# Moving fill units, gate work and mixed rows in a two-block transformer kernel: the recurrence, the MLA pairs and the first half of WO0

## What is computed

```python
proj = rms_norm(x, g_mix) @ w_in      # q_mla, c_kv, k_rope, q/k/v/a/r of GLA, q_mem, gate_logits
kv   = rms_norm(c_kv, g_ckv) @ w_ukv  # k_nope and v of MLA
o_mla = causal_block_attention(q_full, k_full, v_mla, 192 ** -0.5)      # 8 heads
og    = gla_chunked(qg, kg, vg, log_a)                                  # 4 heads, a decayed recurrence
o_gla = rms_norm(og, g_gla_out) * silu(r_gla)
o_mem = softmax attention over mem                                      # 4 heads
gates = sigmoid(gate_logits + b_gate).reshape(B, S, 3, D_MODEL)
y = gates[..., 0, :] * o_mla + gates[..., 1, :] * o_gla + gates[..., 2, :] * o_mem
x = x + y @ w_o
```

## Time and profile before

| | us |
|---|---|
| median of 3 runs | 972.43 (970.01 to 975.63) |
| profiled execution | 970.61 |
| its span, first to last instruction | 969.0 |
| PE busy in it | 919.7 |
| DVE busy | 736.7 |
| ACT busy | 540.2 |
| mean granted clock of PE (1 is 2.4 GHz) | 0.989 |

### The profile page before, as it was taken

One profiled execution on the slowest core, in us unless ns is written; L12 is line 12 of the kernel. 1 busy time (PEld: TensorE's weight loads), 2 busy tenths in 40 slices (PEclk: granted clock), 3 DMA queues, 4 the chain that ended last, 5 costly groups with the idle time before them and its releaser, 6 DMA issues.

```text
span 969.0 us, 13749 instructions
## 1 busy us (share of the span) xinstructions
PE 919.7 (95%) x4684; PEld 737.8 (76%) x4684; DVE 736.7 (76%) x1048; ACT 540.2 (56%) x815; POOL 158.3 (16%) x247
## 2 busy tenths in 40 slices
PE   6999999998989799999999999989999899999996
PEld 5787787786866587888888887756777688888885
DVE  5787456878466777888687878875668879999977
ACT  6567654465766545555433344677754666666631
POOL 8000000124600000011021100380000013333300
PEclk9999999998999899999999999999999999999999
DMA  8674633676552334888678955322224745555571
GB/s 259 226 232 149 191 118 125 229 269 205 158 168 76 109 119 158 278 262 270 206 267 297 326 174 195 114 81 76 88 93 140 224 152 173 174 174 179 180 256 57
DMA packets 100035, 175.12 MB, mean 181 GB/s; under 512 B 8284, under 2 KB 36476, under 8 KB 99980
## 3 DMA queue, kind: packets, MB, share of 16 engines
q1 hardware_dynamic: 92748, 148.87, 47.5%
q0 software_dynamic: 7184, 25.50, 8.0%
q10 hardware_dynamic: 48, 0.04, 0.0%
HBM read 173.33 MB, written 1.05 MB: 180 GB/s over the span
## 4 chain that ended last, share of the span: by engine, by line
PE 73%; DVE 14%; ACT 7%; issue 4%; DMA 1%; DVEq 0%; SPq 0%; ACTq 0%
PE acc L736 61%; DVE wlo L1809 4%; ACT whi L1338 2%; PE turned L1206 1%; PE turned L829 1%; DMA raw<-in_w_mem_kv 1%; PE turned L1304 1%; PE scores L1195 1%; PE scores L975 1%; PE turned L772 1%; DVE turn L1864 1%; DVE soft L2451 1%; PE turned L1095 1%; PE turned L941 1%; PE turned L1118 1%
## 5 line engine op out<-in xcount | busy, mean ns | idle before, releaser
L1809 DVE TENSOR_TENSOR wlo<-raw,whi 128x1024 fp32r<-128x1024 f32 (+2 forms) x270 | 344.5, 1297 | 102.4 <-ACT whi L1338 92.3
L1338 ACT CAST whi<-raw 128x1024 fp32r<-128x1024 f32 (+2 forms) x270 | 273.6, 1030 | 182.8 <-PE acc L736 143.5
L736 PE MATMUL acc<-whi,lta_lo 128*128 128x512 f32 (+2 forms) x576 | 230.6, 400 | 8.1 <-DVE lta_lo L1849 6.8
L736 PE MATMUL acc<-wlo,lta_hi 128*128 128x512 f32 (+2 forms) x576 | 222.6, 386 | 0.0
L736 PE MATMUL acc<-whi,lta_hi 128*128 128x512 f32 (+2 forms) x576 | 222.5, 386 | 0.0
L736 PEld LDWEIGHTS acc<-whi,lta_lo 128*128 128x128 f32 x576 | 108.7, 189 | 45.5 <-issue 13.6
L736 PEld LDWEIGHTS acc<-wlo,lta_hi 128*128 128x128 f32 x576 | 108.5, 188 | 22.3
L736 PEld LDWEIGHTS acc<-whi,lta_hi 128*128 128x128 f32 x576 | 108.9, 189 | 19.1
L736 PE MATMUL acc<-whi,ltb_lo 128*128 128x512 f32 (+1 forms) x272 | 107.7, 396 | 6.3 <-DVE ltb_lo L2579 2.4
L643 POOL DMA_DIRECT2D wm<-in_w_mod x48 | 34.4, 719 | 465.4 <-DVEq L1909 267.0
L736 PE MATMUL acc<-wlo,ltb_hi 128*128 128x512 f32 (+1 forms) x272 | 104.5, 384 | 0.0
(11 more groups left out here) (349 smaller groups left out, 1332.2 us busy)
## 6 DMA issues: line engine op xcount, KB each, us to landing
raw<-in_w_in SPq DMA_DIRECT2D x88, 512.0 KB, 3.9
wm<-in_w_mod POOLq DMA_DIRECT2D x48, 512.0 KB, 5.5
raw<-in_w_up SPq DMA_DIRECT2D x88, 256.0 KB, 3.0
raw<-in_w_up SPq DMA_DIRECT2D x32, 512.0 KB, 4.4
raw<-in_w_down SPq DMA_DIRECT2D x32, 512.0 KB, 5.1
raw<-in_w_down SPq DMA_DIRECT2D x44, 256.0 KB, 3.0
raw<-in_w_mem_kv SPq DMA_DIRECT2D x8, 512.0 KB, 5.9
raw<-in_w_o SPq DMA_DIRECT2D x8, 512.0 KB, 4.1
```

The costliest lines, as they stand in the source:

```text
L736: ins = pe.matmul(acc[s][:, t, 0:n], lhs[part][:, kt0 + kk, tok], w[:, u % RING, kk, 0:n], start=(k == 0 and kk == 0 and j == 0), stop=(la ...
L1338: act.copy(whi[:, s, :, 0:n], raw[:, s, :, 0:n]).then_inc(hi_ready, 1)
L1809: dve.tensor_tensor(wlo[:, s, :, 0:n], raw[:, s, :, 0:n], whi[:, s, :, 0:n].bitcast(F32), ALU.subtract)\
```

## The change

It moves work and adds no computation:

- Of the 16 fill units of the recurrence, the two of s = 0 go behind the turns of gqT and of gkT, one each. DVE gets an `ahead(u0)` before its first exponents.
- UKV0 goes ahead of the outputs go.0 to go.3. DVE makes the last modulation row and the last weights before the split and the bias of G21.
- MLA's fill units are 2, 2, 2, 2, 0 per pair (with the one before the first turn) instead of 1, 2, 1, 2, 2.
- G11 and G00 are both biased and sigmoided in pair 0; DVE multiplies by G11 at the start of pair 1, by G00 at its end, and biases G01 in pair 2. ACT's sigmoid of G01 comes after its casts of y.0 and y.1.
- The mixed rows of pairs 0 and 1 are signalled together, those of pair 2 and of pair 3 each alone (`mix_pair`). y.0 and y.1 are turned ahead of O3, y.2 and y.3 between the token halves of WO0.1.

```diff
 def mla_units(j):
-    return (1, 3, 4, 6, 8)[min(j, MLA_PAIRS)]
+    return (2, 4, 6, 8, 8)[min(j, MLA_PAIRS)]
...
-    out += pairs_t("MLA", MLA_PAIRS)
-    out += g("y", 4) + g("hc", 4) + g("h2", 4)
+    out += pairs_t("MLA", MLA_PAIRS, ahead={MLA_PAIRS - 1: g("y", 4)[:2]})
+    out += g("y", 4)[2:] + g("hc", 4) + g("h2", 4)
...
-            for name, src in (("gqT", gq), ("gkT", gk)):
+            qg = ["Q1", "Q2", "G20", "G21"]
+            for j, (name, src) in enumerate((("gqT", gq), ("gkT", gk))):
                 turn_tokens(name, src, 4)
+                fill(qg, j, 1)
...
-                if s < 8:
+                if 1 <= s < 8:
                     fill(qg, 2 * s, 2)
...
+            pe.wait_ge(ev("ckT_ready"), 1)
+            unit("UKV0", 0, ckT)
             for name in ("gla.off", "gla.7.0", "gla.7.1"):
...
             def mla_fill(p):
                 for j in range(mla_units(p - 1) if p else 0, mla_units(p)):
                     unit(f"G0{j // 4}", j % 4, lta)
+                if p == MLA_PAIRS:
+                    turn_mixed((0, 1), 1)
+            def turn_mixed(groups, mixed):
+                pe.wait_ge(ev("branches_mixed"), mixed)
+                turn_tokens("y", r_gla, groups=groups)
...
-            turn_tokens("y", r_gla, ready="branches_mixed", groups=(0, 1))
             for k in range(4):
-                if k == 1:
-                    turn_tokens("y", r_gla, ready="branches_mixed", groups=(2, 3))
                 lt_wait("y", k)
-                unit("WO0", k, lta)
+                for t in range(T):
+                    unit("WO0", k, lta, tokens=(t,))
+                    if k == 1:
+                        turn_mixed((2 + t,), 2 + t)
...
             def mla_after(p):                       # ACT
-                if p in (0, 1, 3):
-                    gate(("G11", "G00", "G01")[(p + 1) // 2])
+                if p == 0:
+                    gate("G11")
+                    gate("G00")
+                elif p == MLA_PAIRS - 1:
+                    lt_act("y", lta, (0, 1))
+                    gate("G01")
...
             done(dve.memset(attn, 0.0))
+            ahead(u0)
             dve.wait_ge(ev("gmask_ready"), 1)
...
                 if s < 8:
                     exponents(s + 1)
+                else:
+                    mod_row(3)
+                    weights(8)
                 ahead(u0 + 2 * s)
...
             mod_out(3)
-            weights(8)
...
+            def mla_before(p):                      # DVE
                 if p == 1:
                     gate_on("G11", r_gla)
+            def mla_turned(p):
+                if p == MLA_PAIRS - 1:
+                    lt_dve("y", lta, groups=(0, 1))
+            def mla_after(p):
+                if p == 0:
+                    gate_in_psum("G11")
+                    gate_in_psum("G00")
+                elif p == 1:
                     done(dve.tensor_tensor(r_gla, r_gla, o_mem, ALU.add))
+                    b, k = T_USE["MLA.O1"]
+                    dve.wait_ge(t_free[b], k + 2)
+                    gate_on("G00", o_mla)
+                    part = slice(0, COLS)
+                    done(dve.tensor_tensor(r_gla[:, :, part], r_gla[:, :, part], o_mla[:, :, part], ALU.add))
+                    dve.sem_inc(ev("branches_mixed"), 1)
                 elif p == 2:
-                    mix(0)
-                if p in (0, 1, 3):
-                    gate_in_psum(("G11", "G00", "G01")[(p + 1) // 2])
+                    gate_in_psum("G01")
```

More of the change, by code:

```diff
@@ L196, in attention_t, with pairs_t @@
     return out
-def pairs_t(name, n, extra={}):
+def pairs_t(name, n, extra={}, ahead={}):
     out = []
     for p in range(n):
-        out += [f"{name}.PT{2 * p}", f"{name}.PT{2 * p + 1}", f"{name}.O{p}"] + extra.get(p, [])
+        out += [f"{name}.PT{2 * p}", f"{name}.PT{2 * p + 1}"] + ahead.get(p, []) + [f"{name}.O{p}"] + extra.get(p, [])
     return out
@@ L958, in _ @@
                 pe.wait_ge(t_free[b], k + 2)
-            qg = ["Q1", "Q2", "G20", "G21"]
             for s in range(9):
@@ L997, in _ @@
                     ins.then_inc(full, 1)
-            pe.wait_ge(ev("ckT_ready"), 1)
-            for c in range(4):
+            for c in range(1, 4):
                 unit(f"UKV{c}", 0, ckT)
@@ L1588, in mla_after @@
             def mla_after(p):
-                if p in (0, 1, 3):
-                    gate(("G11", "G00", "G01")[(p + 1) // 2])
+                if p == 0:
[4 more added lines that the diff above has]
+                    gate("G01")
             attend_pairs("MLA", MLA_PAIRS, mla_exps, PLAN.unit["G00"], mla_units, 3, after=mla_after)
-            lt_act("y", lta)
+            lt_act("y", lta, (2, 3))
             ahead(PLAN.unit["WO1"])
@@ L1958, in attend, with attend_pairs @@
                         after(i)
-            def attend_pairs(name, n, maxima, sums, weigh, first, units, after=None, early_sums=False):
+            def attend_pairs(name, n, maxima, sums, weigh, first, units, after=None, early_sums=False,
+                             before=None, before_weighing=None):
                 def rows_of(p):
@@ L1980, in attend_pairs @@
                 for p in range(n):
+                    if before:
+                        before(p)
                     if early_sums:
@@ L1987, in attend_pairs @@
                         inverses(p)
+                    if before_weighing:
+                        before_weighing(p)
                     b, k = T_USE[f"{name}.O{p}"]
@@ L2264, in _ @@
                     gate_on("G20", o_mem)
-                if s % 2 == 0:
+                if s % 2 == 0 and s < 8:
                     mod_row(s // 2 - 1)
-                elif s >= 3:
+                elif s in (3, 5, 7):
                     mod_out(s // 2 - 1)
             mod_out(3)
-            weights(8)
             dve.wait_ge(ev("qq_sq"), 2 * T * H_MLA)
@@ L2315, in mla_maxima, with mix_pair @@
                 return neg(s, 2, (NOPE + ROPE) ** -0.5)
-            def mla_after(p):
+            def mla_before(p):
                 if p == 1:
                     gate_on("G11", r_gla)
-                    done(dve.tensor_tensor(r_gla, r_gla, o_mem, ALU.add))
-                elif p == 2:
-                    mix(0)
-                if p in (0, 1, 3):
-                    gate_in_psum(("G11", "G00", "G01")[(p + 1) // 2])
-            def mix(c):
-                part = slice(COLS * c, COLS * c + COLS)
-                b, k = T_USE[f"MLA.O{MLA_PAIRS // 2 * (c + 1) - 1}"]
-                dve.wait_ge(t_free[b], k + 2)
-                gate_on(f"G0{c}", o_mla)
+            def mla_turned(p):
[6 more added lines that the diff above has]
+                elif p == 1:
+                    done(dve.tensor_tensor(r_gla, r_gla, o_mem, ALU.add))
+                    b, k = T_USE["MLA.O1"]
[4 more added lines that the diff above has]
+                    dve.sem_inc(ev("branches_mixed"), 1)
+                elif p == 2:
+                    gate_in_psum("G01")
+            def mix_pair(p):
+                b, k = T_USE[f"MLA.O{p}"]
+                dve.wait_ge(t_free[b], k + 2)
+                dve.wait_ge(gate_sig, n_gate["G01"] + 1)
+                first = 256 * (p % 2)
+                part = slice(256 * p, 256 * p + 256)
+                ins = dve.tensor_tensor(o_mla[:, :, part], o_mla[:, :, part],
+                                        acc[PLAN.bank("G01")[0]][:, :, first:first + 256], ALU.mult)
+                if p == MLA_PAIRS - 1:
+                    frees("G01", ins)
+                else:
+                    done(ins)
                 done(dve.tensor_tensor(r_gla[:, :, part], r_gla[:, :, part], o_mla[:, :, part], ALU.add))
@@ L2340, in mla_weigh @@
                 return ins
-            attend_pairs("MLA", MLA_PAIRS, mla_maxima, sums_of_pair, mla_weigh, PLAN.unit["G00"], mla_units, mla_after)
-            lt_dve("y", lta, groups=(0, 1))
-            mix(1)
+            attend_pairs("MLA", MLA_PAIRS, mla_maxima, sums_of_pair, mla_weigh, PLAN.unit["G00"], mla_units, mla_after,
+                         before=mla_before, before_weighing=mla_turned)
+            for g in (2, 3):
+                mix_pair(g)
             lt_dve("y", lta, groups=(2, 3))
```

## The result

The changed kernel takes 973.42 us (median; 971.64 to 975.28), the kernel before 970.03 us (968.88 to 975.63). The ratio is 1.0039, with a 95% interval of 1.003 to 1.0048: some 3.8 us slower, where 0.3 us faster was forecast. The profiled execution took 974.51 us, with a span of 972.9.

The account below looks back on a forecast made before the run. PE was taken as the bound, busy 919.7 of 969.0 us, plus its waits and low clock. Terms -2.7 - 1.3 + 3.7 = -0.3 us, from a median of 972.43, gave 972.1 us, range 966 to 978.

Parts of the forecast that it names:

- four new waits: Signs on PE: about 1 us before L968, 3 between output matmuls, 5 in MLA pair 1, 1 before WO0.2.
- part C: MLA, the mixing and WO0: a loss of 3.7 us, bounds a gain of 1 to a loss of 9.
- part A: Fill units behind the turns of gqT and gkT: a gain of 2.7 us, bounds 1.0 to 4.0.
- The group for the off-diagonal part (L967) waits for them and starts at 165.3: Recurrence start: the group waits 1 us for DVE's two products, ready at about 165.1; it stood at 168.06 before.
- Part B: End of the recurrence, UKV0 ahead of the outputs: a gain of 1.3 us, bounds 3.2 to -0.3.
- the drop with the smaller price: End of the recurrence: a clock drop behind the 3.0 us wait in the outputs, counted at 1.7 us.
- Rival 1: MLA pair 1: no wait for G11's bank, 4.4 us less wait and 1.5 of clock, 966.2 us; chance 0.15.
- The clock is low there as before: MLA's end: WO0.0 starts 2.4 us later, with the low clock there costing what it did before.
- Rival 2: Clock stays up through the 3 us wait in Part B, returns sooner in part C: 968.9 us; chance 0.12.
- Rival 3: MLA: PE's clock does not come back between the waits, 5.6 us more, 977.7 us; chance 0.15.
- Rival 4: Fills of part A and Part B only move the wait, so part C alone counts: 976.1 us; chance 0.07.
- The rule on tables: ACT: two table loads fewer, as a rival 2.6 us less, 969.5 us (966.8 by the skill's figure); chance 0.03.

Follow-up runs that it names:

- a_only: Kernel before plus only the fill units behind the gqT and gkT turns and DVE's ahead(u0): 969.76 us, ratio 0.9988.
- B alone: Kernel before plus only UKV0 ahead of the outputs and DVE's last modulation row and weights ahead of split and G21 bias: 966.91 us, ratio 0.9966.
- after_g11: Changed kernel with DVE multiplying by G11 right behind its sigmoid, ahead of the splits and G00's bias: 967.53 us, 0.9963 of the kernel before.
- C alone: Kernel before plus only the changes to MLA, the mixing and WO0: 976.34 us, ratio 1.0066.
- ab_god: Kernel before plus part A and Part B, with DVE copying go.0 and go.1 out: 966.53 us, 0.9968 of the kernel before.

## Why the prediction was wrong, step by step

The forecast had the places and three of the four new waits right, and the sign wrong. In the two traces of before and after the 4.2 us of the miss are 1.9 from part C, where the low clock at O3 and WO0 was taken to cost what it cost before; 1.6 from a fall of the clock near 750 that the sum had at nothing; and 0.6 from part A, where a group of scores was to wait for its operands alone.

**Part A: forecast -2.7, measured -2.06 in the trace and -1.2 by the ratio of a_only (0 to -2.3).** The step "The group for the off-diagonal part (L967) waits for them and starts at 165.3" failed first. The products were ready at 165.14, as forecast (165.1). But the group also needs the bank of the scores, which DVE's first predicated copy of weights(0) empties, and that stands behind the products:

```profile
163.72 0.69 DVE L2239 TENSOR_TENSOR arena<-arena 128x512 f32<-128x512 f32 x1 [1.04 <-ACT arena L1536]
164.45 0.69 DVE L2241 TENSOR_TENSOR arena<-arena 128x512 f32<-128x512 f32 x1
165.17 1.50 DVE L2263 COPY_PREDICATED arena<-ident,scores 128x512 f32<-128x512 int32 x2
```

That is 0.7 us. The larger fault is the base: the price of the scores at half speed in the earlier trace rows was taken as the program's. Against the usual 11.1 us from T to O, A gains 0.46 us; the other 1.6 were there in one trace of three. That A's -2.06 came near the forecast was luck of this one trace of before.

**Part B: forecast -1.3, measured -1.26 in the trace.** The wait of 3.0 and the drop with the smaller price came as put. The step was right against a base with 3.4 us lost. But all 1.3 us are clock, and the kernel before had the smaller loss too in one trace of three; so the exact number was in part luck. In the medians B alone gave 3.0 us, more than any of these traces accounts for: its median granted clock over the executions is 0.994, against 0.991 before. 0.003 of 966 us is 2.9 us less lost, which agrees in size; at which places stays open.

**Part C: forecast +3.7, measured +5.56 (4.9 to 6.3 over five traces).** The term of the wait was right: 4.8 forecast, 4.86 measured, and so was the place of the multiplication in DVE's queue, behind the splits and the bias. Rival 1 priced the edit that takes it away at 4.4 us of wait and 1.5 of clock, 5.9 in all; after_g11 came out 5.9 us below the changed kernel by the medians (7.4 by the ratios, 5.6 to 7.0 from M to L). The mis-sized term is "The clock is low there as before" at O3 and WO0. Before, most of that stretch fell in the wait of 5.04 us. Now PE works through it: O3 took 338.29 - 335.73 = 2.56 us where 1.33 is usual, 1.2 us that the forecast had at nothing. WO0.0 was to be 2.4 us late and was 4.1 (338.29 - 281.67 from M, against 337.45 - 284.94). The other 0.5 us was there earlier: O1, behind G01.0 and G01.1, started 35.15 us from M, where the forecast's sum gives 34.66, and 0.37 of that is the time of these two units, which lost more than the 1.5 us put for them. WO0.2 then was at 65.83 us from M, where it was 60.43 before and 64.2 in the forecast.

**The late clock: not forecast, +1.61.** The sum counted a drop only behind waits that the change makes. A wait that it leaves alone can be followed by one too: in three of four traces here, in none of three before. Whether the changed kernel meets it more often, or these few traces only happen to, stays open, and so does the cause; its share of the 3.4 us between the medians can't be separated from A's and B's.

**Rivals.** Rival 1 did not happen and was right as a price. Rival 2, the clock staying up, did not happen; in C it stayed low for longer. Rival 3 asked whether the clock comes back between the waits: it did, in all four traces, and was low again from 332 to 336 on. Rival 4 is near the measured time for the wrong reason: A and B were not worth nothing, they gave 2.1 us together, and C alone cost 6.4. The rule on tables had no effect that can be seen: the two loads left ACT's count (815 to 813 instructions), and no wait of PE ended earlier for it.

**The numbers.** The outcome that had the chance of 0.65, within 0.5%, came true; the forecast's base, 972.43 us, was a median of three executions and 2.4 us above the one of twenty. With 970.03 the same sum gives 969.7, and the miss is 3.7 us, not the 1.3 that 972.1 suggests.

## What to carry to other kernels

Where a stretch of low clock in one trace is a term of the sum, look for the waits that precede it and price it from none to twice its loss: it is the part of a trace that the next execution doesn't repeat, and a wait that is hidden in it, or that hides it, changes what an edit is worth. When fill units are pulled forward, ask for each who frees the bank that it will write, and give the instruction that does so the first place in its queue; two such orders on DVE were worth 5.9 us and 1 to 2 us here. Ask also which engine is idle when a bank is to be emptied: moving the copies ahead in the busy engine's queue cost about 2 us here, giving them to the idle one gained 1 to 2, each near the noise in time but plain in the waits.

## What the runs showed of the hardware

- The clock fell behind waits of 1.80 us (at 750 in the changed kernel) and 1.83 us (at 166 to 171 in a_only), and stayed up behind the same two waits in other executions. It stayed up behind 1.60 us in ab_god. Behind 2.93 us (eight traces) and 4.86 us (five) it was low every time. A fall lost 1.7 or 3.4 us of clock; what lay in a wait cost no time.
- DVE's split of one tile (two inputs from SBUF) took 1.18 us in the MLA pairs, with POOL idle, and a median of 1.76 (1.58 to 3.19) in ab_god between 242 and 254 us, with POOL at work. The one of 3.19 us is the split that UKV3 waited for; it explains the 1.60 us. That POOL is the reason is argued, not tested. The Trainium skill, GPSIMD Engine Reference, section "1. Specifications", names an interface shared with VectorE that contends where an instruction has two SBUF inputs; the two medians agree with it.
